# x turned into separate bank pairs with idle products ahead, score products in pairs, and ranking read from PSUM, in a three-stage transformer kernel on one core

## The reference

```python
def first_block(...):
    xn = rmsnorm(h, norm_mix[l])
    h = h + token_mixer(xn, ...)            # xn @ w_in, 8 forgetting + 8 dilated heads, @ w_out
    h = h + hierarchical_moe(rmsnorm(h, norm_ffn[l]), ...)

def second_block(...):
    for l in range(2):
        h = modulate(x, norm_mix[l], sh_m, sc_m)
        y = even_mixer(...) if l % 2 == 0 else odd_mixer(h, conv_w_in, conv_w, conv_w_out)
        x = x + g_m * y
        x = x + g_f * ec_moe(modulate(x, norm_ffn[l], sh_f, sc_f), ...)

def ec_moe(h, w_router, w_gate, w_up, w_down):
    cap = 2 * n // 16                        # 32 tokens per expert
    aff = softmax(h @ w_router)
    g, idx = top_k(aff.swapaxes(1, 2), cap)
```

## Time and profile before

| what | us |
|---|---|
| median of three runs | 1963.01 (1961.33 to 1964.66) |
| profiled execution, its own time | 1957.78 |
| its span | 1956.0 |
| PE busy, share of the span | 1455.3 (74%) |
| DVE, ACT, POOL busy | 490.1, 239.1, 82.9 |
| chain that ended last: DMA, PE, DVE | 56%, 31%, 5% |
| bytes moved, mean rate | 717.52 MB, 367 GB/s |

### The profile page before, as it was taken

The page is one execution under the profiler, slowest core; times in us unless marked ns, Lnnn a source line. Parts: engine busy times, 40 slices in busy tenths (PEclk is TensorE's granted clock), DMA queues, the critical chain, the costliest instruction groups (busy, mean ns, idle before and its releaser), DMA issues.

```text
span 1956.0 us, 28721 instructions
## 1 busy us (share of the span) xinstructions
PE 1455.3 (74%) x12642; PEld 795.2 (41%) x12642; DVE 490.1 (25%) x972; ACT 239.1 (12%) x584; POOL 82.9 (4%) x92
## 2 busy tenths in 40 slices
PE   7998887777687898899666566566999755666655
PEld 3454543333243353556323223223876422323222
DVE  3864421111112058743000000003553100000001
ACT  2122211111211121321000000001001000000000
POOL 1200000000000023100000000000000000000000
PEclk9997999888899999899878888887999987888788
DMA  9543899999999997458999999999986999999997
GB/s 367 182 158 138 309 418 420 418 421 423 420 416 418 414 345 256 152 246 364 419 420 423 420 420 422 419 422 401 349 340 260 419 422 419 422 422 418 424 419 308
DMA packets 122641, 717.52 MB, mean 367 GB/s; under 512 B 5904, under 2 KB 10512, under 8 KB 97808
## 3 DMA queue, kind: packets, MB, share of 16 engines
q1 hardware_dynamic: 121376, 713.24, 89.7%
q10 hardware_dynamic: 1136, 2.36, 0.3%
HBM read 714.54 MB, written 1.05 MB: 366 GB/s over the span
## 4 chain that ended last, share of the span: by engine, by line
DMA 56%; PE 31%; DVE 5%; issue 4%; POOL 2%; ACT 1%; SPq 0%; DVEq 0%; ACTq 0%; POOLq 0%
DMA ring<-in_moe_w_up 38%; DMA ring<-in_w_down 10%; PE bank L2522 4%; PE bank L1610 4%; DMA ring<-in_w_gate 4%; PE bank L502 4%; DMA ring<-in_moe_w_down 3%; PE bank L1601 3%; PE bank L1658 2%; PE bank L942 2%; PE bank L973 1%; PE bank L646 1%; PE bank L2282 1%; DMA ring<-in_attn_w_in 1%; POOL small L275 1%
## 5 line engine op out<-in xcount | busy, mean ns | idle before, releaser
L1610 PE MATMUL bank<-ring,arena 128*32 128x256 f32 x3968 | 296.5, 453 | 177.6 <-DMA ring<-in_moe_w_up 114.2
L1658 PE MATMUL bank<-ring,arena 128*32 128x256 f32 x2944 | 236.5, 476 | 181.1 <-DMA ring<-in_moe_w_down 136.8
L1610 PEld LDWEIGHTS bank<-ring,arena 128*32 128x32 f32 x3968 | 145.7, 125 | 306.7 <-issue 112.9
L1658 PEld LDWEIGHTS bank<-ring,arena 128*32 128x32 f32 x2944 | 114.3, 131 | 293.0 <-issue 160.6
L1601 PE MATMUL bank<-ring,arena 128*32 128x512 f32 x1008 | 136.8, 665 | 57.1 <-DMA ring<-in_w_up 32.1
L502 PE MATMUL bank<-ring,low 128*128 128x512 f32 (+1 forms) x352 | 159.4, 605 | 1.6 <-DVE low L363 1.6
L1730 DVE TENSOR_TENSOR arena<-arena,bank 128x128 f32<-128x128 f32 (+1 forms) x64 | 22.7, 354 | 521.4 <-PE bank L1610 517.9
L1684 PE MATMUL bank<-arena 32*128 32x256 f32 x1024 | 93.5, 435 | 16.7 <-PE bank L1684 10.7
L502 PEld LDWEIGHTS bank<-ring,low 128*128 128x128 f32 x352 | 68.6, 202 | 74.1 <-issue 71.1
L1736 ACT ACTIVATE arena<-bank 128x256 f32<-128x256 f32 x64 | 24.5, 383 | 573.2 <-PE bank L1671 570.5
L1745 DVE TENSOR_TENSOR arena<-bank,gate_strips 128x256 f32<-128x256 f32 x32 | 13.6, 424 | 297.8 <-PE bank L1658 297.8
(11 more groups left out here) (308 smaller groups left out, 1346.5 us busy)
## 6 DMA issues: line engine op xcount, KB each, us to landing
ring<-in_moe_w_gate SPq DMA_DIRECT2D x62, 2048.0 KB, 25.5
ring<-in_moe_w_up SPq DMA_DIRECT2D x62, 2048.0 KB, 26.9
ring<-in_moe_w_down SPq DMA_DIRECT2D x62, 2048.0 KB, 26.8
ring<-in_w_up SPq DMA_DIRECT2D x32, 2048.0 KB, 25.6
ring<-in_w_gate SPq DMA_DIRECT2D x31, 2048.0 KB, 25.4
ring<-in_w_down SPq DMA_DIRECT2D x30, 2048.0 KB, 26.2
ring<-in_ada_w SPq DMA_DIRECT2D x24, 2048.0 KB, 13.6
ring<-in_attn_w_in SPq DMA_DIRECT2D x8, 2048.0 KB, 21.1
```

The lines of the kernel that those rows point to most:

```text
L1610: last = nc.tensor.matmul(GU[up][32 * j:32 * j + 32, 0:QW], xgT[:, x + kk, a:a + C], w[:, kq, j * QW:(j + 1) * QW], start=(kk == 0), stop= ...
L1658: last = nc.tensor.matmul(z_bank(M)[32 * j:32 * j + 32, 0:QW], act_s[:, b, q * C:(q + 1) * C], w[:, kq, j * QW:(j + 1) * QW], start=(kk == ...
```

## The change

- **x in two transfers.** Each tile of x has a transfer and a semaphore of its own. ScalarE, which norms tile 0, waits for the first; VectorE, which norms tile 1, for the second. To stay within the number of semaphores, two others (`on_loaded`, `on_turned`) become one.
- **Stage one.** TensorE starts with 26 idle products into bank 2. Tile 0 is then turned in banks 4 and 5, tile 1 in banks 6 and 7, both ahead of unit 0. `tr_pe` is unchanged.
- **Stage three.** 14 idle products stand ahead of the turning; tile 0 is turned in banks 0 and 1, tile 1 in banks 2 and 3. `tr_pe` is unchanged here too.
- **Idle products** multiply a column of -0.5, broadcast to 128 x 128, by itself, and no longer the identity.
- **Scores.** At an even step, TensorE issues products u and u + 1 together; at an odd step none. The pair waits until the maximum of product u - 1 has been read.
- **Ranking.** The copy L1428 is gone; the first maximum and the first replacement read bank 1. 25 idle products stand beside the ranking where there were 27.

```diff
-FILL = (20, 5, 5, 27)
+FILL = (20, 5, 5, 25, 26, 14)
+        GB = [bank[0:2], bank[2:4]]
+        IDLE = [bank[2], bank[5], bank[3]]
+        some = minus_half[:, 0:1].broadcast_to([P, P])
+        def keep_pe(n, b=0):
+            for _ in range(n):
+                nc.tensor.matmul(IDLE[b][:, 0:P], some, some, start=True, stop=True)
...
         def scores_pe(u):
             if u >= 2:
-                pe.wait_ge(at_m, u - 1)
+                pe.wait_ge(at_m, u)
...
+            for n in range(2):
+                a = HD * n
+                nc.tensor.matmul(bank[2 + n][:, 0:w], qT[br][a:a + HD, hd // 2, t * P:(t + 1) * P],
+                                 kT[br][a:a + HD, hd // 2, 0:w], start=True, stop=True).then_inc(at_s, 1)
...
         def block1_pe():
+            pe.wait_ge(setup_done, 1)
+            keep_pe(FILL[4])
             pe.wait_ge(first_loaded, 32)
-            tr_pe(0, 0, xn_ready(0, 0))
+            tr_pe(0, 0, xn_ready(0, 0), AB)
+            tr_pe(0, 1, xn_ready(0, 1))
...
                 elif what == "scores":
-                    scores_pe(i)
+                    if i % 2 == 0:
+                        scores_pe(i)
...
-            dve_step(v.tensor_copy(workT, bank[1][0:E2, 0:S]))
+            left = bank[1][0:E2, 0:S]
             for n in range(CAP // 8):
-                dve_step(v.max(best8, workT))
-                dve_step(v.match_replace(workT, best8, workT, -1.0))
+                dve_step(v.max(best8, left))
+                dve_step(v.match_replace(workT, best8, left, -1.0))
+                left = workT
...
         def odd_pe():
+            keep_pe(FILL[5])
             for t in range(T):
-                tr_pe(4, t, xn_ready(4, t), ZB)
+                tr_pe(4, t, xn_ready(4, t), GB[t])
...
-            sp.dma_start(xn[:, :, :], x[0].rearrange("(t p) d -> p t d", p=P)).then_inc(x_loaded, 16)
+            for t in range(T):
+                sp.dma_start(xn[:, t, :], x[0, t * P:(t + 1) * P, :]).then_inc(x_loaded[t], 16)
```

More of the change, by code:

```diff
@@ L1284, in transformer_blocks @@
         LG = [bank[1], bank[0]]
-        IDLE = [bank[2], bank[5]]
         shift_row = router_sb[:, 0, E2:2 * E2]
-        def keep_pe(n, b=0):
-            for _ in range(n):
-                nc.tensor.matmul(IDLE[b][:, 0:P], ident, ident, start=True, stop=True)
         def logits_pe(m, c0, n, banks):
@@ L2534, in odd_act @@
             load_strips_act(1)
[L2535 removed]
+            for t in range(T):
+                tr_act(4, t, hT, mod[:, 1, 1, :], mod[:, 1, 0, :], GB[t])
             for n in range(2):
@@ L2547, in odd_dve @@
             norm_dve(4, h, 4, ready)
-            both_dve(4, hT, mod[:, 1, 1, :], mod[:, 1, 0, :], ZB)
+            for t in range(T):
+                tr_dve(4, t, hT, mod[:, 1, 1, :], mod[:, 1, 0, :], GB[t])
             dve_step(v.memset(zp[:, :, 0:1], 0.0))
```

37 lines of the change are left out of this document (15 added, 22 removed).

## The result

| | us | ratio to the kernel before, 95% interval |
|---|---|---|
| before, median of four runs beside it | 1962.88 (1961.33 to 1964.66) | |
| changed, median of four runs | 1948.43 (1946.57 to 1950.42) | 0.9926 [0.9909, 0.9943] |
| changed, profiled execution; its span | 1949.03; 1947.2 | |

The change makes the kernel 14.5 us (0.74%) faster. The quotient of two medians can differ from the ratio given beside them, by up to 0.0011 here. The forecast was 1953.6 and its range ended at 1948.5, 0.1 us above the result. The two profiled executions lie only 8.75 us apart (1957.78 and 1949.03), which is a second thing to explain.

A forecast was written before the change was run, and what follows sets the result against it. Prediction: stage one bound by its chain, mostly TensorE; mixtures' transfers wait for TensorE's first expert, so gains pass on in full. -4.6 - 3.7 - 0.8 - 0.3 = -9.4 from 1963.0 gave 1953.6 us, range 1948.5 to 1960.

The forecast's parts named there:

- Start, -4.6: Start of stage one: forget gates at 19.95 us instead of 24.60, 4.6 us won; bounds -2.7 and -5.
- Rival 2: Start of stage one: the clock falls between idle products and unit 0, start only -2.7, time 1955.5 us; chance 0.13.
- Rival 4: Idle products: constant columns don't raise the clock as the identity did, +11.2 us, time 1974.2; chance 0.06.
- Pairs, -3.7: Attention scores: pairing removes 16 of 32 products, a step-by-step list sums to -3.7 us; bounds +2.3 and -6.
- steps 13 and 14: Attention scores: TensorE itself is late at step 13, so its removed product wins 0.63 us.
- steps 9 and 15: Attention scores: TensorE itself is late here, so each removed product wins 0.63 us.
- step 3: Attention scores: TensorE itself is late here, so the removed product wins 0.42 us.
- Step 25 likewise, at the lower clock: Attention, ahead of a chain of section sums: the removed product wins 1.15 us at the lower clock.
- Rival 3: Attention: waits cost less and lower-clock stretches shrink, attention -7, sum -12.7 us, time 1950.3; chance 0.07.
- steps 2 and 8: Attention: pairs wait for a maximum behind the sums of units 6 and 8, losing 1.9 and 0.4 us.
- Ranking, -0.8: Both rankings: idle products bind, two fewer and no copy win 0.4 us each; bounds -0.4 and -1.2.
- Stage three, -0.3: Start of stage three: first projection no earlier, give or take 0.5 us, term -0.3; bounds +1.2 and -3.4.

The follow-up runs named there:

- no_idle_start: The changed kernel without the 26 idle products at the start; 1949.65 us, ratio 0.9946 to the kernel before.
- copy: The kernel before, run again with no edit; 1961.96 us, ratio 0.9998 to the kernel before.
- changed, again: The changed kernel, run again with no edit; 1950.00 us, ratio 0.9951 to the kernel before.
- early_overlap: Changed kernel with maxima 1 and 7 ahead of the sums of units 6 and 8, and no wait for tile 0's copies; 1941.66 us, ratio 0.9904.
- before_keep: The kernel before plus 16 idle products, 8 ahead of each of the modulation's third and fourth section sums; 1957.26 us, ratio 0.9988.
- keep_attention: The changed kernel plus 28 idle products at four places in attention; 1944.53 us, ratio 0.9926 to the kernel before.
- best: Changed kernel with early_overlap's two edits and 16 idle products ahead of the modulation's third and fourth section sums; 1937.56 us, ratio 0.9896.

## Why the prediction was right or wrong

**Direction and mechanisms: right.** All four parts act where the forecast put them. The gains reached the first expert, as forecast, but for 0.4 us of lower clock behind the last output product; behind the expert the spread of the next stretch (494.4 to 498.8 us) hides whether all of it is kept. The gates' distance to the first section sum is 49.0 for 49.1.

**Start, -4.6: right.** -5.0 in the trace and -5.7 by timing alone. Idle products end at 8.75 for 9.2; unit 0 starts 0.44 early, its weights having landed at 12.5. Rival 2 fell: after 1.3 us of waiting and two sets of transposes unit 0 ran wholly at the upper clock. The Trainium skill, page "TensorE: Matmul & The Clock Gate", section "Part 4: PE-mode transpose", has it that the upper level doesn't engage for transposes; by that the clock should have been down. The trace does not agree: eight transposes took 1.13 us at the upper level, and in no_idle_start the clock came up 1.8 us into unit 0, behind 3.9 us of transposes. Rival 4, that a constant doesn't raise the clock, fell with the first transposes: 1.13 us for eight behind constant idle products, 1.94 without them. What I had not seen is that the idle products bring only 1.0 of it.

**Pairs, -3.7: the places were right, the term was too small.** This is the step that failed. It measured 6.4 us in the two traces (-0.7 and -5.7) and 7.1 by timing alone. Two things were missing.

First, each removed product was priced too low. The distance between two half projections with steps 13 and 14 between them, before and changed:

```profile
119.60 3.65 PE L502 MATMUL bank<-ring,low 128*128 128x512 f32 x8
...
126.31 3.65 PE L502 MATMUL bank<-ring,low 128*128 128x512 f32 x8
```

```profile
115.33 3.65 PE L504 MATMUL bank<-ring,low 128*128 128x512 f32 x8
...
121.27 3.65 PE L504 MATMUL bank<-ring,low 128*128 128x512 f32 x8
```

That is 6.71 and 5.94 us, 0.77 for a step that the list has at 0.63; steps 9 and 15 gave 0.77 too, and step 3 gave 0.57 for 0.42. So the steps where TensorE was late won 2.9 for 2.3. The losses were as forecast: 1.8 for 1.9 at unit 6, and 0.4 at unit 8, where the wait itself was 1.14 us but step 7, which the list doesn't name, gave most of the rest back. In all -0.7 for 0. In the second half, at one clock, 3.9 stands against the list's 3.2; that it looks so near the forecast's 3.7 is luck.

Second, the clock. What I left out stands in "Step 25 likewise, at the lower clock": I took the lower stretches of before as fixed and priced one step in them. They are not. The stretch from bias to last output product in every profiled execution, with its time at the lower level (us):

| execution | bias to last output product | of it at the lower clock |
|---|---|---|
| before, copy, ranking alone, stage three alone | 77.4, 77.4, 77.4, 77.4 | 27.3 |
| start alone | 74.6 | 20.5 |
| pairs alone | 70.1 | 20.5 |
| no idle start | 72.0 | 23.9 |
| changed | 71.7 | 23.9 |
| changed, again | 67.9 | 17.1 |
| early_overlap | 67.9 | 17.1 |
| before_keep (16 idle products in it) | 75.5 | 20.5 |
| keep_attention (28) | 69.1 | 10.2 |
| best (16) | 67.9 | 10.2 |

Where pairs and no pairs had the same 20.5 us of lower clock, they lie 4.5 apart. Between before and start alone, the same work is 2.8 us shorter with 6.8 us less of it; between the two executions of the changed kernel 3.8 with 6.8 less. So without added products a microsecond less of lower clock gave back 0.4 to 0.6. Of the -5.7 here, 3.9 to 4.5 are the pairs and 1.2 to 1.8 the clock; of the -7.4 in pairs alone, 3.9 to 4.5 and 2.9 to 3.5. How much of the clock's part the pairs bring about stays open, since start alone has a shorter stretch as well. Where idle products had bought the clock, less came back: best has 6.8 us less of lower clock than early_overlap and the same 67.9.

Rival 3 named this, with attention at -7, and I gave it 0.07, as an afterthought to a list of waits, when the rows already showed 27 us of attention at the lower level. Its reason was only half right: the waits at steps 2 and 8 did not shrink. Its time of 1950.3 is nearest to the first result, 1948.43; but its -12.7 is further from the later set's -10.7 between medians (1950.00 against 1960.67) than the forecast's -9.4.

**Ranking, -0.8: right.** In the ranking alone 0.5 us in the first and 0.3 in the second, for 0.4 each; in the changed kernel 0.6 and 1.1. That holds only with the clock up: in the changed kernel's later execution the 25 idle products beside the first ranking took 7.33 us for 5.76, and from them to the gather it was 8.75 us for 7.19.

**Stage three, -0.3: right.** Nothing by timing; the first projection stands 6.18 us behind the first transpose, as before. The clock rose 2.8 us after its start instead of 4.3, but 6.0 us after it in the later execution of the same kernel.

**The base.** I set the sum against a median of three, 1963.01. Larger sets of the kernel before gave 1961.56, 1960.67 and 1961.70; on those the forecast would have been 1.3 to 2.3 us lower. But the four runs of before beside the result itself had 1962.88, so the base does not explain the 14.5. The two sets of the changed kernel differ too: -9.4 us is a ratio of 0.9952, which is what the later set measured (0.9951), and 5 us short of the first. So part of the miss is the spread of a set of four, and where the later set meets the forecast's sum, it is partly luck: stage one alone was 11.1 and 16.3 us ahead at its first expert in the two traces, for 8.3. The range was too narrow for that: it allowed 1.8 us for spread, while the 35 executions of the kernel before span 13 us, and two profiled executions of the changed kernel differ by 5.2 at the first expert. What remains open is what draws the clock: no run here could hold it fixed for a whole execution.

## What to carry to other kernels

A cost list made by summing instruction times has one clock in it; where the trace shows stretches at the lower clock next to the edited work, ask for each whether the edit moves its end, and give that its own term and range. Work removed beside such stretches can be worth more than its own time (7.1 us by timing here, for some 4.5 at one clock). A few idle products in the waits that set a stretch off can take the stretch away, though here the timing alone did not prove a gain by it, while the same products put where there is no wait, or where the clock is already low, cost more than they bring. Separate buffers are worth nothing until the wait that they make needless is removed as well, and a pair formed from two steps inherits the later of their waits: look at what stands ahead of its releaser on that engine. And one profiled execution cannot carry a difference of a few microseconds when two of the same kernel differ by five.

## What the runs showed of the hardware

- Transposes and short waits held the clock: unit 0 started at the upper level though from 8.75 to 12.56 us there was nothing but 1.13 + 1.12 us of transposes and 0.38 + 1.30 us of idle time.
- In the copy of before, the clock fell at 167.9 us although no single wait in the stretch ahead of it was over 1.90 us, and TensorE was busy 4.10 of its 6.80 us:

```profile
161.00:167.80 6.80, 4.10 (x28) 3.40 (x28) 5.86 (x13) 2.44 (x9) 0.00 (x0) 1.00 0.01 2
```

- The same kernel has its lower stretches in the same places in four executions of one form of attention (before, copy, ranking alone, stage three alone: 13.7 us each, beginning between 167.3 and 167.9 us), and in different ones in two executions of another (changed: 158.2 to 168.5 us; again: 156.6 to 163.4).
- Two products of 64 rows in different halves of the array cost as one, 0.49 us for four records with 128 keys and 0.70 with 256, where one product has 0.48 and 0.70, in every kernel with pairs run here, at the upper clock.
- A first MAX8 and MATCH_REPLACE8 that read PSUM took 0.42 and 0.40 us, as from on-chip memory.
